# Thirteen full-size f32 matmuls of constants put ahead of small matmuls in the hybrid mixer of a two-model block kernel

## The reference, cut to what matters

```python
    kk = jnp.where(strict, jnp.einsum('bhncd,bhnsd->bhncs', k, k) * ratio, 0.0)
    a_mat = jnp.eye(c, dtype=jnp.float32) + beta[..., None] * kk
    ...
    u_v = lax.linalg.triangular_solve(a_mat, beta[..., None] * v, ...)
    w_k = lax.linalg.triangular_solve(a_mat, (beta * gamma)[..., None] * k, ...)
    ...
    def step(state, inp):
        u = uv_n - jnp.einsum('bhcd,bhdv->bhcv', w_n, state)
        o = jnp.einsum('bhcd,bhdv->bhcv', qg_n, state) + jnp.einsum('bhcs,bhsv->bhcv', qk_n, u)
        state = cd_n[..., None, None] * state + jnp.einsum('bhcd,bhcv->bhdv', kt_n, u)
```

```python
        decay = jnp.exp(jnp.where(causal, diff, -jnp.inf))
        scores = jnp.einsum('bhcd,bhsd,bhcsd->bhcs', q_n, k_n, decay)
        o = jnp.einsum('bhcs,bhsv->bhcv', scores, v_n) + ...
```

## Time and profile before

| | |
|---|---|
| median of 3 runs | 2460.06 us (2458.47 to 2465.06) |
| the profiled execution's own time | 2461.06 us |
| its span, first to last instruction | 2459.3 us |
| TensorE matmul busy | 2359.7 us, 96% |
| VectorE busy | 1683.5 us, 68% |
| ScalarE busy | 681.1 us, 28% |
| mean granted clock of TensorE | 0.972 of full |

### The profile page before, as it was taken

One profiled execution on the slowest core, in us unless ns is written; L12 is line 12 of the kernel. 1 busy time (PEld: TensorE's weight loads), 2 busy tenths in 40 slices (PEclk: granted clock), 3 DMA queues, 4 the chain that ended last, 5 costly groups with the idle time before them and its releaser, 6 DMA issues. The chain is left out here.

```text
span 2459.3 us, 35706 instructions
## 1 busy us (share of the span) xinstructions
PE 2359.7 (96%) x14784; PEld 1911.8 (78%) x14784; DVE 1683.5 (68%) x2643; ACT 681.1 (28%) x1239; POOL 139.2 (6%) x128
## 2 busy tenths in 40 slices
PE   8998859999999999999999899999999999999997
PEld 6886658977888888887755688888888888888886
DVE  6674466756888865558888686666666886666653
ACT  2321363022211101424677503222102113222200
POOL 0000002001000011000211010000010001000001
PEclk9999679999999999999999999999999999999999
DMA  4220003412232364212200171222562541322341
GB/s 180 77 77 3 21 2 129 146 52 78 95 102 94 128 207 145 88 67 82 73 10 2 55 271 65 98 94 95 184 223 89 205 180 61 103 94 95 132 137 65
DMA packets 70193, 252.44 MB, mean 103 GB/s; under 512 B 7792, under 2 KB 8080, under 8 KB 69520
## 3 DMA queue, kind: packets, MB, share of 16 engines
q1 hardware_dynamic: 69744, 249.63, 29.9%
q10 hardware_dynamic: 288, 0.54, 0.1%
HBM read 248.04 MB, written 2.10 MB: 102 GB/s over the span
## 5 line engine op out<-in xcount | busy, mean ns | idle before, releaser
L385 PE MATMUL psum<-rounded_n,rounded_high 128*128 128x512 f32 x1856 | 739.0, 398 | 4.4 <-DVE rounded_n_low L539 1.8
L386 PE MATMUL psum<-rounded_n_low,rounded_high 128*128 128x512 f32 x1856 | 726.3, 391 | 0.0
L387 PE MATMUL psum<-rounded_n,rounded_ring 128*128 128x512 f32 x1856 | 726.2, 391 | 0.0
L339 DVE TENSOR_TENSOR rounded_ring<-ring,rounded_high 128x1024 fp32r<-128x1024 f32 (+1 forms) x360 | 445.7, 1238 | 43.5 <-ACT rounded_high L322 31.5
L385 PEld LDWEIGHTS psum<-rounded_n,rounded_high 128*128 128x128 f32 x1856 | 350.6, 189 | 85.2 <-issue 7.2
L386 PEld LDWEIGHTS psum<-rounded_n_low,rounded_high 128*128 128x128 f32 x1856 | 350.7, 189 | 76.5 <-issue 5.5
L387 PEld LDWEIGHTS psum<-rounded_n,rounded_ring 128*128 128x128 f32 x1856 | 350.4, 189 | 73.7
L337 DVE CAST rounded_high<-ring 128x1024 fp32r<-128x1024 f32 (+1 forms) x347 | 248.8, 717 | 187.3 <-PE psum L387 180.1
L385 PE MATMUL psum<-rounded_arena,rounded_high 128*128 128x512 f32 x720 | 281.3, 391 | 4.4 <-DVE rounded_ring L339 4.4
L387 PE MATMUL psum<-rounded_arena,rounded_ring 128*128 128x512 f32 x720 | 281.0, 390 | 0.0
L386 PE MATMUL psum<-rounded_arena,rounded_high 128*128 128x512 f32 x720 | 280.9, 390 | 0.0
(11 more groups left out here) (494 smaller groups left out, 2752.4 us busy)
## 6 DMA issues: line engine op xcount, KB each, us to landing
ring<-in_w_up SPq DMA_DIRECT2D x132, 512.0 KB, 3.3
ring<-in_w_down SPq DMA_DIRECT2D x48, 512.0 KB, 3.6
n_low<-in_mod_w SPq DMA_DIRECT2D x48, 512.0 KB, 5.4
arena<-in_mod_w SPq DMA_DIRECT2D x48, 512.0 KB, 5.1
ring<-in_w_ab_in SPq DMA_DIRECT2D x37, 512.0 KB, 3.3
ring<-in_w_mix_in SPq DMA_DIRECT2D x31, 512.0 KB, 3.4
ring<-in_w_sc_in SPq DMA_DIRECT2D x24, 512.0 KB, 4.8
ring<-in_w_down SPq DMA_DIRECT2D x24, 384.0 KB, 3.2
```

The lines of the kernel that those rows point to most:

```text
L339: nc.vector.tensor_tensor(self.rounded(raw), raw, self.rounded(high), ALU.subtract).then_inc(self.weights_split, 1)
L385: self.nc.tensor.matmul(out, w_high, x_high, start=first, stop=False)
L386: self.nc.tensor.matmul(out, w_high, x_low, start=False, stop=False)
L387: return self.nc.tensor.matmul(out, w_low, x_high, start=False, stop=last)
```

## The change

A function `fill(bank, columns)` is new. It issues one full-precision f32 matmul: the 128x128 identity as weights, the first columns of the constant table `decay0` as the moving operand, result into the first columns of a PSUM bank. It is called ahead of the waits of `inverse_times(3)`, `inverse_times(4)`, `inverse_update(3)` and `inverse_update(4)` (256 columns each), `join_first` and `join_second` (512 columns each), and behind the waits of `join_third` (384 columns) and, for unit 0, of `use` at `DIAG` and levels 0 to 4 (256 columns each; here the level's own wait, `qk_ready`, comes after it). That is four, two, one and six, so 13 program matmuls with 3968 columns in all. Every one writes a region that the following matmuls overwrite, and nothing reads its result.

```diff
+        def fill(bank, columns):
+            nc.tensor.matmul(k.psum[:, bank, 0:columns], k.const("ident"), k.const("decay0")[:, 0:columns],
+                             start=True, stop=True)
+
         def inverse_times(n):
+            if n > 2:
+                fill(D0, 2 * P)
             pe.wait_ge(begun, 1)
             pe.wait_ge(inverse, n)
             piecewise(k.psum[:, D0, :], k.an, k.xt).then_inc(crossed, 1)
 
         def inverse_update(n):
+            if n > 2:
+                fill(D0 + 1, 2 * P)
             pe.wait_ge(mixed_up, n)
             piecewise(k.psum[:, D0 + 1, :], k.xn, k.pt).then_inc(copied, 1)
 
         def join_first():
+            fill(D0, T)
             pe.wait_ge(inverse, SMALL_LEVELS)
...
         def join_second():
+            fill(D0 + 1, T)
             pe.wait_ge(joints_kept, 1)
...
             pe.wait_ge(joints_kept, 2)
             pe.wait_ge(quarters, 2)
             pe.wait_ge(ret_weighted, 2 * RETS)
+            fill(D0 + 2, 3 * P)
             for h in range(HEADS):
...
             pe.wait_ge(taken, TURNS + x - (1 if u and 0 <= s < VALUES else 0))
+            if u == 0 and s < BIG:
+                fill(room(u, s), 2 * P)
             if s < BIG:
                 small(u, s)
```

## The result

The changed kernel took 2465.53 us in the median of 20 runs, the kernel before 2462.36 us in 20 runs on the same chip. The ratio is 1.0015 with an interval of 1.0008 to 1.0022: slower by 3.7 us (2.0 to 5.4). That is under the 0.3% that the forecast took for the finest difference to be told, but with 20 runs of each it can be told. The forecast was no change, and 2460 us.

What follows compares the result with a forecast made beforehand. In the mixers it took instruction supply as the bound as much as TensorE's low clock. Terms a to h summed to -0.2 us against 2461.06 us, 2460 us on the median's scale; own range 2457 to 2464, with rivals 2453 to 2466.

Steps and rivals of the forecast that it cites:

- a: Fills of inverse_times(3) and inverse_update(3): covered by instruction waits, 0; bounds 0.94 and -1.5 us.
- b: Fills of inverse_times(4) and inverse_update(4): 0.94 us less an issue wait of 0.47 behind them, +0.5 us.
- c: Fill of join_first: operands are ready, so nothing covers its 512 columns, +0.9 us.
- d: Fill of join_second: outlasts ScalarE's copy by 0.6 us, less some 0.4 from joins at full clock, +0.2 us.
- e: Fills of use(0) to use(3) and join_third: fills and savings vanish in instruction supply, +0.3 us; bounds -5 and +2.7.
- f: Fill of use(4): covered while VectorE computes the crossing's factors, 0; +0.2 us at half clock.
- g: Fill of use(5): +0.47 us against some 0.6 saved by scan_out(0) at full clock; taken as +0.2, half clock +0.94.
- h: From 284 to 301.8 us, without fills: the clock may be high on entry, -2.3 us; bounds -5.5 and 0.
- Rival 1: The clock is high through 302 us, instruction supply still bounds the levels: -3.4 us, 2457 us; chance 0.22.
- Rival 2: Instruction supply is no limit, TensorE's faster work is the whole story: -9.9 us, 2450 us; chance 0.12.
- Rival 3: The clock falls in unit 0 all the same, fills run at half speed: +7.1 us, 2467 us; chance 0.11.

Runs made afterwards that it cites:

- change_and_idle: The whole change plus 128-column matmuls of constants where TensorE waits for data from 279 us to the end of the mixers; 0.9970 against the kernel before.
- levels_double: The changed kernel with unit 0's six level fills at 512 columns each instead of 256; 1.0009 against the kernel before.
- joins_only: The kernel before with only the three fills of the joins; 0.9999 against the kernel before.
- before_again: The kernel before, unchanged, profiled in one further execution; 2459.61 us.
- inverse_only: The kernel before with only the four fills of the inverse levels; 1.0004 against the kernel before.
- levels_twice: The kernel before with levels 0 and 1 of unit 0 issuing their matmuls twice, adding 256 matmuls and 256 loads; 1.0034 against the kernel before.
- idle_units: The kernel before with 128-column matmuls of constants in TensorE's data waits, only from scan_keys(3) at 309 us on; 0.9976 against the kernel before.
- early_fills: The change without its fills of use(2) to use(5), the levels 1 to 4 of unit 0; 1.0003 against the kernel before.
- after_again: The changed kernel, profiled in a second execution; 2465.14 us.
- after_third: The changed kernel, profiled in a third execution; 2463.70 us.
- levels_only: The kernel before with only the six fills of unit 0's diagonal and levels; 1.0008 against the kernel before.

## Why the prediction was wrong, step by step

The steps with their forecast and the mean of three traces of the change, in us. Those of `join_second` to `use(5)` are cut at the end of `join_fourth`.

| step | forecast | measured | how |
|---|---|---|---|
| a, b: inverse levels | +0.5 | -0.5 | -1.3, -0.5, +0.5 against 21.3 |
| c: `join_first` | +0.9 | +1.1 | three times the same |
| d and the first half of e | +0.2 and a part of 0.3 | +1.4 | +0.5, +1.9, +1.7 against 15.5 |
| the rest of e: levels 1 and 2 | the rest of 0.3 | +0.4 | three times the same |
| f: `scan_solve(0)`, level 3 | 0 | 0.0 | -0.1 and +0.2 |
| g: level 4, `use(5)` | +0.2 | +1.2 | three times the same |
| h: 284 to 301.8 us | -2.3 | -1.5 | `scan_keys(1)` to the values, 15.66 to 14.2, three times |
| behind it, to `mix_out` | 0 | 0.0 | +2.9, -1.4, -1.4 |

The forecast summed to -0.2, the trace to +2.1, the whole runs to +3.7 (2.0 to 5.4).

**The step that failed** is e with g: "At full clock the two big joins shrink", and "Both fills and savings vanish in the supply; what is left is the late start from b to d, and 0.3 for the added instructions." It took for granted that the clock, once full, stays full to the end of the levels. It fell back at 267.0 to 269.0 us in the three traces and in change_and_idle, at 267.3 us in levels_double and at 266.7 us in joins_only. In the three traces it falls within the issue wait of 1.7 to 2.0 us in `join_fourth` (268.4 and 267.0 us, waits that end at 268.94 and 267.50) or 1.4 us behind it (268.2, a wait that ends at 266.82). That this wait makes the clock fall is not shown. So e had one join to save on and not two: from the start of the third join with its fill to level 0 takes 2.64 us in all three, where it was 3.60, but the fourth join takes 4.5 to 5.6 us from its start to its end, where it was 3.67, for the issue wait and the half clock behind it.

In g the forecast set 0.47 us of fill against 0.6 us that `scan_out(0)` would save, both at full clock, and took +0.2. Measured is +1.2: the fill takes 1.15 us at half clock, `scan_out(0)` saves nothing, and the wait of 1.36 us behind level 4 covers none of it. It is 4.38 or 4.39 us from `scan_out(0)` to `scan_keys(1)` in seven traces without this fill (before, before_again, inverse_only, joins_only, levels_twice, idle_units, early_fills) and 5.54 or 5.55 in four with it (after, after_again, after_third, levels_only). The forecast had +0.94 as its figure for half clock, so here the clock was wrong and the way right. No run takes out the fill of `use(5)` alone.

What e and f said of the cover held, even at half clock: the fills of levels 1 to 3 cost 0.4 us together. That the supply was a bound is right too (levels_twice: +7.96 us for two blocks), and up to 268 us the blocks came as before in the first trace: at 255.9, 261.0, 264.4 and 268.0 us after, at 255.8, 261.1, 264.6 and 268.0 us before. Behind 268 us they came later after (271.9, 276.0 and 279.8 us) than before (271.6, 275.2 and 278.6 us).

**The rest of d and e** is the same fall seen earlier: +0.5 if more than half of the last 29 records of `join_fourth` run at full clock, as forecast for d and e together (0.5), and +1.7 to +1.9 if the clock falls ahead of them.

**Step a** had the low clock of 237 to 243.8 us as a bound of -1.5 and did not expect it. It was nearly reached in one trace: the first shows a low stretch of 237.5 to 240.9 us only and no wait of 1.95 us, and -1.3 for a and b together. after_again has no low stretch at all between 217 and 268 us and yet only -0.5, and after_third has the whole of it (236.3 to 243.1 us) and +0.5. On average a and b give 0.5 us (0.6 over all traces) where they were to cost 0.5, which is less than the three executions differ.

**Step c** was right, 1.06 us where 0.9 stood: the fill of 512 columns takes 1.13 us as the row shows it, of which the next step covers little.

**Step h** had the sign right and its size near: -1.5 where -2.3 stood. Its way was another. The clock was low on entry at 284 us, and it rose at 295 to 299 us, within the crossings, instead of 301.85. In all three it fell once more for 3.4 to 6.8 us behind that. The last fills of the levels may bring the rise forward: with them it came 9.1 to 9.7 us behind the start of `scan_keys(1)` in five traces (after, after_again, after_third, levels_only, levels_double), without them 17.6 to 20.5 us behind it in six. But inverse_only and levels_twice, without them, have it at 8.9 and 9.4 us. So the cause stays open.

**The rivals.** Rival 1 (the clock high through 302 us) did not come in any trace of the change. Rival 2 (the supply no limit) is refuted by levels_twice and by the spacing of the blocks. Rival 3 is half right: the clock falls in unit 0, and g costs about what it said (1.2 us where 0.9 stood). But its cost for c to g is 4.0 and not 6.6 us, since the third join had its full clock and the issue waits covered more; and the credit of h stands beside it. `scan_out(0)` began at 280.71, 283.92 and 282.50 us: once inside the forecast's sign (0.5 to 2 us after 279.75), twice between it and rival 3's. The first two signs of the forecast were there (clock full for a part, joins at 2.08 us); the third, issue waits that grew, held for the one of 1.99 us and failed for the others (2.5 us in all before, 2.7 after).

Two things stay open. The join fills cost 2.1 to 2.3 us in the trace and nothing in the whole run (0.9999, 0.9990 to 1.0008); its profiled execution was the slowest of its 12 (2467.04 us, median 2464.24), and what gives the price back in the others was not found. And 1.7 us of the change's 4.2 us in profiled spans lie behind `mix_out`; whether the change causes them is not known, since two executions of one kernel differ by 1.3 us there.

## What to carry to other kernels

Fill work for the clock paid where TensorE waits for data and larger tiles follow: the same kind of matmuls gave 0.9954 there, sized to each wait, and 1.0015 ahead of small tiles.

Before counting on "it vanishes in a wait", ask what the wait hangs on. A wait for instructions, or for VectorE work that is already under way, covers a fill put ahead of it: levels 1 to 3 took fills of 3.6 us for 0.4. A wait for work that begins only when TensorE's own next result is there covers nothing: ahead of level 4 one fill cost 1.2 us, and behind level 4, inside the very same wait, four matmuls at full clock left 0.29 us of it.

And a clock that has risen is a state to be priced on both sides at each wait that stays.

## What the runs showed of the hardware

- Instructions come in blocks of about 253, and from 218 to 290 us they begin 3.25 us or more apart in every trace, at either clock: after, with the clock full, 3.4 and 3.6 us apart between 261.0 and 268.0 us. Two blocks more cost 7.96 us.
- Small tiles with a fill among them need not bring the clock back even when TensorE has no gap: in levels_only 6.00 us of 6.00 busy, clock 0.50, with a full-array fill of 256 columns among them. With fills of 512 columns in the levels (levels_double) it rose inside unit 0, at 274.1 us. Full-array fills of 512 columns ahead of the first two joins (384 ahead of the third) kept it full to 267 us and beyond, where it falls at 253.7 to 258.5 us without them. The Trainium skill ("TensorE: Matmul & The Clock Gate", section "Why this matters for your kernels") blames idle gaps between bursts. A fall in or behind the wait of 1.7 to 2.0 us agrees with that in kind, though no run shows that this wait makes it fall; the stretch without a gap at 0.50 does not agree.
- 89 matmuls of constants of 128 columns, mostly in data waits, raised the mean clock of 282 to 368 us from 0.69 to 1.00, which took 9.9 us from the mixers.
- The same kernel's profiled stretch from `scan_keys(1)` to `mix_out` can differ by 4.3 us (94.91 and 90.60), with low stretches of the clock at other places, while the times of these executions are 2464.89, 2465.14 and 2463.70 us.
